# The S5 recurrence of the prompt's 16 chunks on GpSimd, beside the sample's 64 chunks on VectorE

## The reference

```python
bu = B_bar @ u[t]                       # complex, B_bar from the discretisation
s[t] = a * s[t-1] + bu                  # a complex, per group and state
y[t] = Re(C @ s[t])                     # then + D*u, GELU, GLU, w_out
```

## Time and profile before

| | us |
|---|---|
| median of 3 runs | 1875.8 |
| lowest and highest | 1870.94, 1879.12 |
| profiled execution, its own time | 1876.33 |
| span of its trace | 1874.4 |
| TensorE busy in the span | 1698.6 (91%) |
| VectorE busy | 955.0 (51%) |
| ScalarE busy | 580.3 (31%) |
| GpSimd busy | 232.2 (12%) |

### The profile page before, as it was taken

The page is one execution under the profiler, slowest core; times in us unless marked ns, Lnnn a source line. Parts: engine busy times, 40 slices in busy tenths (PEclk is TensorE's granted clock), DMA queues, the critical chain, the costliest instruction groups (busy, mean ns, idle before and its releaser), DMA issues. The chain is left out here.

```text
span 1874.4 us, 29544 instructions
## 1 busy us (share of the span) xinstructions
PE 1698.6 (91%) x11660; PEld 1564.5 (83%) x11660; DVE 955.0 (51%) x1732; ACT 580.3 (31%) x906; POOL 232.2 (12%) x219
## 2 busy tenths in 40 slices
PE   4997997989999999999898647899989999999996
PEld 2993345979999999999898107899989999999996
DVE  1437666687752675366942990132683232233248
ACT  3225554344222231222623123232243212211221
POOL 0000122212531253130020021000000000000000
PEclk8997998989999999999895668999989999999998
DMA  9422663313433343233195565432223232232212
GB/s 295 117 76 77 204 230 67 75 46 109 129 114 93 116 143 107 82 105 106 45 247 135 181 203 143 110 90 67 68 68 90 67 90 68 67 90 68 62 51 57
DMA packets 273183, 204.35 MB, mean 109 GB/s; under 512 B 30840, under 2 KB 238832, under 8 KB 273072
## 3 DMA queue, kind: packets, MB, share of 16 engines
q1 hardware_dynamic: 238656, 161.40, 29.7%
q10 hardware_dynamic: 27632, 24.72, 4.6%
q0 software_dynamic: 6784, 16.66, 3.4%
HBM read 178.10 MB, written 24.64 MB: 108 GB/s over the span
## 5 line engine op out<-in xcount | busy, mean ns | idle before, releaser
L488 PE MATMUL PS<-XH,WH 128*128 128x320 f32 x2112 | 489.0, 313 | 20.8 <-DVE XL L1015 8.3
L488 PE MATMUL PS<-XL,WH 128*128 128x320 f32 x2112 | 485.5, 311 | 0.0
L488 PE MATMUL PS<-XH,WL 128*128 128x320 f32 x2112 | 485.5, 311 | 0.0
L488 PEld LDWEIGHTS PS<-XH,WH 128*128 128x128 f32 x2112 | 357.2, 190 | 22.3 <-issue 10.4
L453 ACT ACTIVATE WH<-RAW 128x1024 fp32r<-128x1024 f32 x188 | 198.2, 1057 | 556.1 <-PE PS L488 548.2
L488 PEld LDWEIGHTS PS<-XL,WH 128*128 128x128 f32 x2112 | 357.7, 190 | 0.0
L488 PEld LDWEIGHTS PS<-XH,WL 128*128 128x128 f32 x2112 | 357.0, 190 | 0.0
L707 DVE TENSOR_TENSOR HT<-PS,GT 128x640 f32<-128x640 f32 x52 | 42.9, 824 | 421.1 <-PE PS L488 419.0
L458 DVE TENSOR_TENSOR WL<-RAW,WH 128x1024 fp32r<-128x1024 f32 x188 | 244.5, 1326 | 4.8 <-ACT WH L453 3.7
L488 PE MATMUL PS<-HH,WH 128*128 128x320 f32 x832 | 190.5, 310 | 0.0
L488 PE MATMUL PS<-HH,WL 128*128 128x320 f32 x832 | 189.6, 309 | 0.0
(11 more groups left out here) (254 smaller groups left out, 1737.0 us busy)
## 6 DMA issues: line engine op xcount, KB each, us to landing
RAW<-in_ffn_w SPq DMA_DIRECT2D x120, 512.0 KB
RAW<-in_w_ada SPq DMA_DIRECT2D x84, 512.0 KB
c_scratch<-G ACTq DMA_DIRECT2D x32, 256.0 KB, 3.4
b_scratch<-BP ACTq DMA_DIRECT2D x16, 512.0 KB, 2.6
BT<-b_scratch POOLq DMA_DIRECT2D x8, 1024.0 KB, 5.3
RAW<-in_ssm_w_glu SPq DMA_DIRECT2D x16, 512.0 KB
CPL<-c_scratch SPq DMA_DIRECT2D x8, 1024.0 KB, 5.3
ADA<-in_w_ada SPq DMA_DIRECT2D x12, 512.0 KB
```

The costliest lines, as they stand in the source:

```text
L488: ins = nc.tensor.matmul(PS[:, 2 * u + h, 0:HALF], w[:, u, k, :], m[:, k, HALF * h:HALF * h + HALF], start=start, stop=stop)
```

## The change

GpSimd gets a function that computes the 16 steps of the prompt. It is called in `pool_ssm`, after the loads of BT and before `pool_ada(3)`. VectorE computes the sample's 64 steps alone, with 128x128 operations throughout, in a loop of four trips, and waits for GpSimd's last step before FINS. The prompt uses halves 1 of SC1 and SC2, the sample halves 0.

```diff
+        scan_p = sem("s5_scan_p")
...
                 load_bt(T)
+            pool_scan_prompt(g)
             pool_ada(3)
...
+        def pool_scan_prompt(g):
+
+            g.wait_ge(inc_a, 2 * NB)
+            g.wait_ge(inc_v, 2 * NB)
+            for s in range(1, CCH + 1):
+                c = 4 * (s - 1)
+                t1, t2 = SC1[:, 1], SC2[:, 1]
+                g.tensor_tensor(t1, ST[:, s - 1], AR[:, :, :], ALU.mult).then_inc(scan_p, 1)
+                g.tensor_tensor(t2[:, ::-1, :], ST[:, s - 1], AI[:, :, :], ALU.mult).then_inc(scan_p, 1)
+                g.wait_ge(scan_p, c + 1)
+                g.tensor_tensor(ST[:, s], ST[:, s], t1, ALU.add).then_inc(scan_p, 1)
+                g.wait_ge(scan_p, c + 3)
+                g.tensor_tensor(ST[:, s], ST[:, s], t2, ALU.add).then_inc(scan_p, 1)
+                g.wait_ge(scan_p, c + 4)
...
-            UN = 16
-            c = run(CCH // UN, 1, 2, 0)
-            run((LCH - CCH) // UN, 2 * CCH + 2, 1, c)
+            with loop(v, LCH // UN) as i:
+                for u in range(UN):
+                    c = 4 * UN * i + 4 * u
+                    s = CCH + 2 + UN * i + u
+                    last, now = ST[:, bass.ds(s - 1, 1)], ST[:, bass.ds(s, 1)]
...
+                    t1, t2 = SC1[:, 0:1], SC2[:, 0:1]
...
+            v.wait_ge(scan_p, 4 * CCH)
             v.tensor_copy(FINS[:, :, :], ST[:, CCH, :, :]).then_inc(scan_done, 1)
```

More of the change, by code:

```diff
@@ L1763, in act_ssm @@
                 a.activation(XH[:, m, :], YIN[:, m, :], ACT.Copy).then_inc(gelu_hi, 1)
+        UN = 16
+        def pool_scan_prompt(g):
[11 more added lines that the diff above has]
+                g.wait_ge(scan_p, c + 4)
         def dve_ssm():
@@ L1775, in dve_ssm @@
             v.wait_ge(inc_v, 2 * NB)
[L1777 to L1800, removed]
@@ L1802, in dve_ssm @@
-            UN = 16
-            c = run(CCH // UN, 1, 2, 0)
-            run((LCH - CCH) // UN, 2 * CCH + 2, 1, c)
+            with loop(v, LCH // UN) as i:
[3 more added lines that the diff above has]
+                    last, now = ST[:, bass.ds(s - 1, 1)], ST[:, bass.ds(s, 1)]
+                    shape = [P, 1, 2, GROUPS]
+                    ar = AR[:, :, :].unsqueeze(1).to_broadcast(shape)
+                    ai = AI[:, :, :].unsqueeze(1).to_broadcast(shape)
+                    t1, t2 = SC1[:, 0:1], SC2[:, 0:1]
+                    v.tensor_tensor(t1, last, ar, ALU.mult).then_inc(scan_t, 1)
+                    v.tensor_tensor(t2[:, :, ::-1, :], last, ai, ALU.mult).then_inc(scan_t, 1)
+                    v.wait_ge(scan_t, c + 1)
+                    v.tensor_tensor(now, now, t1, ALU.add).then_inc(scan_t, 1)
+                    v.wait_ge(scan_t, c + 3)
+                    v.tensor_tensor(now, now, t2, ALU.add).then_inc(scan_t, 1)
+                    v.wait_ge(scan_t, c + 4)
```

## The result

| | us |
|---|---|
| kernel before, median of 4 runs | 1874.78 (1870.94 to 1879.12) |
| changed kernel, median of 4 runs | 1887.06 (1884.46 to 1888.43) |
| ratio, with 95% interval | 1.0063 (1.0038 to 1.0089) |
| profiled execution, its own time, and its span | 1884.46, 1882.6 |

The changed kernel is slower by 0.63%, 12.3 us between the medians. I had forecast 1902 us, 26 us more than the profiled run before. The direction was right and 1887 us lies in the stated range, just inside its lower end, but the change is less than half of the forecast one. So the question for the experiments is not only whether the mechanism is the stated one, but where the other 14 us went.

A forecast was written before the change was run, and what follows sets the result against it. The adaLN chain, with its stores and MT loads in GpSimd's queue, bounds the stage. A 42 us scan ahead of it gives +22 us at the fold, +4 us for a stopped store, +26 us in all: 1902 us, range 1886 to 1921.

The forecast's parts named there:

- The path: adaLN chain through TensorE groups, ScalarE ROWS, GpSimd stores, then MT, releases TensorE's next stage; its start moves the end one for one.
- The removal on VectorE: VectorE's recurrence would end 7.7 us sooner undisturbed; nothing on the path waits for that, so worth at most 9.0 us.
- GpSimd's scan: 64 operations ahead of group 16's store, 0.54 us a link: 34.6 us with VectorE silent, 42 us taken, range 34.6 to 53.
- The two together: GpSimd and VectorE hold each other up during the scan: GpSimd's scan taken as 42 us, VectorE losing 11 us.
- GpSimd wins: Case in which GpSimd wins the race against VectorE's second operation each time: its scan lasts 34.6 us.
- VectorE wins: Case in which VectorE wins that race each time: 0.14 us more per GpSimd operation, scan 43.6 us.
- The first landing and group 18: After the scan, group 16's store lets ROWS 17 go at 1081.7 us, 33.7 late; ROWS 18 at 1088.7, 30.9 late.
- The MT stall: GpSimd's eight MT loads, held up by VectorE's ENT copies, would take 3.84 us instead of 12.84; fold 22 us late.
- The copies hit a store: VectorE's 12.65 us of copies would stop a GpSimd row store, delaying the chain 0 to 9 us; 4 us taken.
- The second: Rival: GpSimd scan of 20 to 30 us through less fixed cost, 0 to +10 us, 1881 us; 6 in 100.
- The third: Rival: GpSimd loses the port repeatedly (scan 72 us) or fixed cost 0.5 us; +45 us and more, 1925 us; 12 in 100.
- the range of my own terms: Scan of 34.6 us without a stopped store, 1891 us, to 53 us with one of 9 us, 1918 us; 77 in 100.

The follow-up runs named there:

- e1: Changed kernel with GpSimd doing two scan steps behind each adaLN group's row stores instead of all sixteen ahead of group 16's: 1873.36 us, ratio 0.9986 to the kernel before.
- e3: Changed kernel with part 3's row stores issued by ScalarE and its MT loads by SyncE: 1868.65 us, ratio 0.9951 to the kernel before.
- e5: Kernel before with 50 dependent 128x512 memsets on GpSimd ahead of part 3's row stores: 1883.04 us, ratio 1.0029 to the kernel before.
- e7: Changed kernel with 16 more steps of the same four operations on a spare tile, on GpSimd ahead of the row stores: 1922.4 us in one run.
- e9: Kernel before with VectorE's ENT copies waiting until the eight MT loads have landed: 1867.92 us, ratio 0.9951 to the kernel before.
- e3b: Kernel before, its recurrence unchanged, with part 3's row stores issued by ScalarE and MT loads by SyncE: 1867.9 us, ratio 0.9948 to the kernel before.
- e4: Changed kernel with VectorE waiting for GpSimd's 64 operations before its own scan, so the two never run together: 1886.83 us in one run.
- e8: Changed kernel with VectorE's ENT copies waiting until the eight MT loads have landed: 1885.22 us, ratio 1.0047 to the kernel before.
- e2: Kernel before with part 3's eight MT loads issued by SyncE instead of GpSimd: 1867.11 us, ratio 0.9946 to the kernel before.
- e6: Changed kernel with 8 scan steps ahead of group 16's store and one behind each group's stores: 1880.71 us, ratio 1.0023 to the kernel before.

## Why the prediction was right or wrong

**The path** was read rightly: TensorE released by MT, MT by the row stores, these behind GpSimd's scan. The idle time of TensorE behind group 17 is in the place forecast, though 20.8 us and not 35; e1 and e3 take the chain away from the scan and the loss is gone; e5 delays the stores without the scan and has a loss; e7, a single run, doubles the delay and has it one for one at ROWS 18. That the end of the stage moves one for one with the fold nearly holds in e7 (against the changed kernel the fold is 31.3 us later, the stage 30.8 us longer) and in e9 (against the kernel before 9.1 us earlier and 9.8 shorter), but not in e1 (9.4 and 3.6).

**The removal on VectorE brings nothing**: right. The slower steps cost VectorE more than the removal saved it, as forecast. e3 against e3b: 6.7 us of VectorE's end make no difference beyond about 4.5 us either way. In e4, 16 us later, its end does cost.

**GpSimd's scan** is the step that failed, and the largest: 42 us taken, 34.6 to 53 us as its range, 31.7 us measured, below even its lower end. An operation of 128 elements was well read from the rows of 512 and 1024 (0.46 us; 0.453 alone). But I added the gap between dependent operations to all 64, and something for other waits. Two operations without a wait between them overlap: 1030.73 and 1031.15 are 0.42 us apart at a duration of 0.45, and only two of the four in a step have a gap. A link alone is 30.1 / 64 = 0.47 us, not 0.54. That is 4.5 us.

**The two together**: I left the race open between "GpSimd wins" and "VectorE wins" and took the middle, 7.4 us. GpSimd wins each time; it gives up 1.6 us. VectorE loses 14 us where I had 11. The Trainium skill's rule (SBUF — State Buffer, "SBUF: two separate sides"), that the two exclude each other for the whole instruction, would give 53 us for the scan by my estimate. The trace does not agree. It shows the engines holding each other up, but not for the whole instruction: durations of 0.453 us (e4) and 0.293 us alone, 0.746 together, fit in a pair of 0.496 us.

**The first landing and group 18**: 5.6 us taken from issue to ROWS 17, 2.4 measured; 7.0 us from there to ROWS 18, 4.4 measured, since TensorE's sixteen matmuls took 3.64 us, not 6.2. Both durations of mine came from a time in which the weight loads ran beside them: the DMA engines were 0.5 busy in the 6.2 us and 0.02 in the 3.64. The clock is not the reason, as the granted clock was 0.50 in the 3.64 us, the lower of its two levels, after 20.8 us of idle time, and 0.72 on average in the 6.2 of group 18 before. After this stop the loads had run ahead and were over, and the first links behind it were faster than in the steady state.

Together (4.5 + 5.8 for the scan, 3.2 + 2.6 for the first landing and group 18), ROWS 18 was 14.9 us late instead of 30.9. These 16 us are nearly all of the error: the fold came 9.4 us late instead of 26.

**Behind that** 51.0 us for the five periods became 52.5. The MT stall went, as said (3.95 for 12.84 us). The copies hit a store, which I had given 4 us; it was the last, and cost 1.5 us net (e8). The y stage took 65.7 us instead of 64.0 from fold to GLU, with TensorE busy 54.3 and 52.5 us at a mean granted clock of 0.91 and 0.95. In the other runs it lies between 63 and 71 us, the longest, e1 and e4, at the lowest clock, 0.87 and 0.86.

**The rivals**: none was right. The second, small operations with less fixed cost, is the nearest in time (1881 us), but the fixed cost was as read. The third was priced too low: by the rule of the sum, the scan less 20 us, 72 us would be +52 and not +45. The range held the time only because it had been widened for the rivals at its lower end, which is luck: the range of my own terms ended at 1891 us. A small slip that changes nothing: at its own pace VectorE needs 2 x (1.05 + 0.16) = 2.4 us for the two subtractions, not 2.3.

## What to carry to other kernels

Before work is put on an engine that looks idle, list what its queue holds behind the place, DMA issues above all: here GpSimd was busy 12% and its queue carried the critical chain. If the work must go there, put it behind the issues in small pieces: ahead of them the scan cost 0.6%, spread out it was no slower than the kernel before. It was no gain either, and 0.4% slower than the kernels that lose the stall without it (e2, e9). And look for copies on VectorE beside DMA issues from GpSimd: holding the copies back by a wait was worth 0.5%, more than moving the recurrence brought in any run here.

When a delay is priced through a chain, don't take the steady-state durations for its first links without a look at what runs beside them.

## What the runs showed of the hardware

- Two-input operations of VectorE and GpSimd, both 128x128 in fp32 from SBUF, alternate one for one, with a pair in 0.496 us: GpSimd slowed by 5% (30.1 to 31.7 us), VectorE by 80% (1.98 us a step instead of 1.10 in the single steps of the kernel before). Alone, the two operations last 0.453 and 0.293 us.
- A row store of GpSimd lets ROWS go 2.4 us after its issue when the store comes 30 us or more into the stage, with group 18's weights loaded (2.5 us in e4, 2.4 in e7 and e8; 2.8 in e5 at 29.5 us), and 6.8 us after it in e6, where it comes at 16 us and the DMA engines are fully busy.
- VectorE's ENT copies held an issue from GpSimd until they were over in four traces: 9.40 us before and 7.38 us in the changed kernel, over 0.11 and 0.09 us after the last copy, and in the stopped stores of e5 (4.62 us for two issues) and e7 (10.52 us). In e6 they did not: MT loads were being issued when the copies began at 1126.73, and all eight took 5.75 us, over at 1130.06, 9.4 us before the copies' end. The Trainium skill (SBUF — State Buffer, "SBUF: two separate sides") has such issues locked out while VectorE copies in its two-port mode; the four traces agree, e6 does only in part. What sets it apart is open.
